# First modulation in eight groups of two K tiles, with the forget keys and the mix copies moved

## The reference, cut to what matters

```
mod    = silu(c) @ w_ada + b_ada              # one vector for latent, one for context
h      = x * (1 + sc1) + sh1                  # first modulation, both streams
u      = h @ w_in                             # values, keys, forget gates, queries, mix, gates
y_a    = rms_norm(gated linear recurrence(q, k, logf, v)) * silu(g)
y_b    = pooling(u);   y_c = attention(u)
x1     = layer_norm(alpha * x + g1 * (sum_j sigmoid(gate_j) * (y_j @ w_branch_j)) @ w_out)
out    = layer_norm(alpha * x1 + g2 * (relu(h2 @ w_ff1) ** 2) @ w_ff2),   h2 = x1 * (1 + sc2) + sh2
```

## Time and profile before

| | us |
|---|---|
| three runs | 1932.26, 1930.51, 1928.32 (median 1930.51) |
| profiled execution, its own time | 1933.53 |
| its span in the trace | 1931.7 |
| TensorE busy | 1870.1 |

### The profile page before, as it was taken

How to read it: one execution, slowest core, us unless ns; L and a number is a source line. 1 busy time by engine, 2 the same in 40 slices (tenths; PEclk the granted TensorE clock), 3 DMA queues, 4 the chain that set the end, 5 groups by cost and what they waited for, 6 DMA issues and landing times.

```text
span 1931.7 us, 23993 instructions
## 1 busy us (share of the span) xinstructions
PE 1870.1 (97%) x9784; PEld 1562.1 (81%) x9784; DVE 1283.3 (66%) x1454; ACT 810.2 (42%) x971; POOL 277.5 (14%) x165
## 2 busy tenths in 40 slices
PE   5999999999999999999999998999999999999997
PEld 1568987899999887878888887888888888888875
DVE  1236767785868766486676666786676567557786
ACT  1132234464555554444444434543344344434432
POOL 0000000004838253000010100120012001100100
PEclk8999999999999999999999999999999999999999
DMA  9956765554333454385676754565665565656642
GB/s 400 421 223 249 274 218 174 175 175 153 129 134 110 140 209 163 131 288 213 244 273 233 273 198 173 218 237 183 243 246 203 196 218 218 218 196 223 235 168 94
DMA packets 59598, 408.90 MB, mean 212 GB/s; under 512 B 6368, under 2 KB 9056, under 8 KB 10848
## 3 DMA queue, kind: packets, MB, share of 16 engines
q1 hardware_dynamic: 55008, 395.34, 56.0%
q10 hardware_dynamic: 4480, 12.02, 1.7%
HBM read 405.24 MB, written 2.10 MB: 211 GB/s over the span
## 4 chain that ended last, share of the span: by engine, by line
PE 87%; DVE 7%; DMA 2%; issue 1%; POOL 1%; DVEq 1%; ACT 1%; SPq 0%; ACTq 0%
PE main L1423 14%; PE main L1424 14%; PE main L1425 14%; PE side L1400 6%; PE main L1400 6%; PE main L1360 4%; PE main L1362 4%; PE main L1361 4%; PE side L1402 3%; PE main L1402 3%; DVE asum L940 2%; DMA raw<-in_w_ada 2%; PE main L1474 2%; DVE wlo L919 2%; PE main L1476 2%; PE main L1475 2%
## 5 line engine op out<-in xcount | busy, mean ns | idle before, releaser
L919 DVE TENSOR_TENSOR wlo<-raw,whi 128x1024 fp32r<-128x1024 f32 x548 | 703.8, 1311 | 356.4 <-ACT whi L457 355.7
L457 ACT CAST whi<-raw 128x1024 fp32r<-128x1024 f32 x548 | 570.3, 1052 | 745.0 <-PE main L1425 406.6
L1360 PE MATMUL main<-hCL,whi 128*128 128x256 f32 (+1 forms) x768 | 249.0, 324 | 8.0 <-ACT cq L623 4.4
L1362 PE MATMUL main<-hCL,wlo 128*128 128x256 f32 (+1 forms) x768 | 246.0, 320 | 0.0
L1361 PE MATMUL main<-hCL,whi 128*128 128x256 f32 (+1 forms) x768 | 245.8, 320 | 0.0
L940 DVE SCALAR_TENSOR_TENSOR asum<-raw,sm,asum 128x512 f32<-128x512 f32 x240 | 221.8, 924 | 19.5 <-issue 0.4
L1423 PE MATMUL main<-whi,hid 128*128 128x512 f32 x496 | 194.9, 393 | 2.8 <-DVE wlo L919 2.8
L1424 PE MATMUL main<-wlo,hid 128*128 128x512 f32 x496 | 193.1, 389 | 0.0
L1425 PE MATMUL main<-whi,hid 128*128 128x512 f32 x496 | 193.1, 389 | 0.0
L1400 PE MATMUL main<-h,whi 128*128 128x512 f32 x512 | 183.8, 403 | 4.8 <-DVE h L1255 2.5
L1400 PE MATMUL side<-h,whi 128*128 128x512 f32 x512 | 181.3, 399 | 0.0
(11 more groups left out here) (246 smaller groups left out, 2861.6 us busy)
## 6 DMA issues: line engine op xcount, KB each, us to landing
raw<-in_w_f SPq DMA_DIRECT2D x128, 1024.0 KB, 4.9
raw<-in_w_in SPq DMA_DIRECT2D x104, 1024.0 KB, 4.9
raw<-in_w_ada SPq DMA_DIRECT2D x96, 1024.0 KB, 5.5
raw<-in_w_br SPq DMA_DIRECT2D x24, 1024.0 KB, 4.9
raw<-in_w_out SPq DMA_DIRECT2D x16, 1024.0 KB, 4.8
xin<-in_xT SPq DMA_DIRECT2D x4, 1024.0 KB, 15.4
raw<-in_w_ck SPq DMA_DIRECT2D x4, 512.0 KB, 12.9
raw<-in_w_cv SPq DMA_DIRECT2D x2, 1024.0 KB, 4.9
```

Of the source, the lines that this page charges most:

```text
L457: nc.scalar.copy(half_at(q)[0], slots[slot][:, 2 * h:2 * h + 2]).then_inc(hi_made, 1)
L919: TT(half_at(q)[1], slots[slot][:, 2 * h:2 * h + 2], half_at(q)[0].bitcast(F32), ALU.subtract).then_inc(lo_made, 1)
L1360: mm(out, w_hi, x_hi, start=start, stop=False)
L1362: return mm(out, w_lo, x_hi, start=False, stop=stop)
```

## The change

`w_ada` is stored differently for its first 4096 columns (`w_ad1`): a chunk holds eight K tiles of 256 columns. `ada_chunk` makes eight matmuls of 256 columns in place of four of 512, two chunks make 256 sums, and two turns of two matmuls each serve a group of two K tiles, so that there are eight groups of four chunks. The load of the input goes in eight pieces. The values of group `g - 1` follow the four chunks of group `g`, one block behind each, and half of the keys of an earlier group follows them, ahead of the second turn. The last half of the values and the last keys come behind the loop. In the forget stage `keys_turned` and `states` come one chunk later each. In the mix stage the tanh and the copies stand ahead of the exponential of their step. The core of the diff:

```diff
@@ stream()
-    for kc in range(4):
+    for g in range(8):
         for k in range(4):
-            st.add("p", "ada", 8 * kc + k, "w_ada", 4 * kc + k)
...
+            if g and g % 2 == 0 and k == 2:
+                panel("vals", 0, g // 2, "w_in", 4 * PAN_AI + g // 2)
+            st.add("p", "ada", 4 * g + k, "w_ad1", 2 * (g + 8 * (k // 2)) + k % 2)
+        if g == 0:
+            panel("vals", 0, 0, "w_in", 4 * PAN_AI)
+        if g % 2:
+            st.add("s", "keys", g // 2, "w_ck", g // 2, halves=1)
@@ SyncE
-                if name == "ada" and k % 8 == 4:
...
+                if name == "ada" and k % 4 == 2:
+                    kt = 2 * (k // 4)
+                    sp.dma_start(xin[:, kt:kt + 2].rearrange("p k v t -> p (k v t)"),
+                                 xT[:, kt * 2 * T:(kt + 2) * 2 * T]).then_inc(x_in[k // 4], 16)
@@ ScalarE, opening
+            for g in range(8):
+                sums_out(2 * g)
+                if g and g % 2 == 0:
+                    split("vals", g // 2)
+                sums_out(2 * g + 1)
...
+                modulated(g)
+                if g == 0:
+                    split("vals", 0)
+                if g % 2:
+                    split("keys", g // 2)
@@ ScalarE, forget (the same shift by one in query: 0 and 1 become 1 and 2)
-                    if it >= 2 and k == 0:
+                    if it >= 2 and k == 1:
                         key_copy(it - 2)
-                    if it >= 2 and k == 1:
+                    if it >= 2 and k == 2:
                         state_copy(it - 2)
@@ ScalarE, mix (the same lines stood behind the exponential and the square before)
+                    if k == 3:
+                        for b in range(4):
+                            blk("mix", 12 * i, b)
+                            A(ya[:, i * 4 + b], main[:, b, 0:T], ACT.Tanh, scale=0.5).then_inc(gs_sig, 1)
+                    if k == 7:
+                        for b in range(4):
+                            blk("mix", 12 * i + 4, b)
+                            nc.scalar.copy(cq[:, i * 4 + b], main[:, b, 0:T]).then_inc(freed["A"], 1)
                     if k < 9:
                         act.wait_ge(lv_arg, i * 9 + k + 1)
@@ VectorE, opening
+            for g in range(8):
+                if g and g % 2 == 0:
+                    split("vals", g // 2)
+                mods_out(g)
+                modulate(g)
...
@@ TensorE, ada_chunk
-                for j in range(CK):
-                    group = slice(32 * j, 32 * j + 32)
-                    last = mm(side[group, 1], sR[:, k * CK + j], slots[slot][:, j], start=k == 0, stop=k == 3,
-                              tile_position=(0, 32 * j), skip_group_check=True)
+                for j in range(8):
+                    group, first = slice(32 * (j % 4), 32 * (j % 4) + 32), 256 * (j % 2)
+                    last = mm(side[group, 1, 256 * (p % 2):256 * (p % 2) + 256], sR[:, 8 * k + j],
+                              slots[slot][:, j // 2, first:first + 256], start=k == 0 and j < 4, stop=k == 1 and j >= 4,
+                              tile_position=(0, 32 * (j % 4)), skip_group_check=True)
@@ TensorE, opening
+            def keys_at(g):
+
+                n, pair = divmod(g - 2, 2)
+                if 0 <= n < 3:
+                    for b in range(2):
+                        key_block(n, 2 * b + pair)
+
+            for g in range(8):
                 for k in range(4):
...
+                    ada_chunk(4 * g + k)
+                    if k == 2:
+                        turn(2 * g)
+                    if g:
+                        n, h = divmod(g - 1, 2)
+                        inputs_ready(n, h)
+                        value_block("vals", n, h, k, half_ready("vals", n, h), 0)
+                keys_at(g)
+                turn(2 * g + 1)
@@ TensorE, between the chunks of the forget stage
                         if it:
                             ada_turn(3 + it)
                         if it >= 2:
-                            states(it - 2)
-                    if k == 3 and it:
-                        keys_turned(it - 1)
+                            keys_turned(it - 2)
+                    if k == 1 and it >= 2:
+                        states(it - 2)
@@ TensorE, query
                 if k == 0:
                     ada_turn(7)
+                    keys_turned(2)
+                if k == 1:
                     states(2)
```

More of the change, by code:

```diff
@@ L110, in panel @@
         while owed:
-            st.add("a", "sum", done, "w_ada", 4 * SUMS[done // 4] + done % 4)
+            st.add("a", "sum", done, "w_ada", 4 * (SUMS[done // 4] - 8) + done % 4)
             done, owed = done + 1, owed - 1
@@ L222, in panels @@
     four = (0, 1, 2, 3)
-    order = [half for n in range(4) for half in (("vals", n, 0), ("vals", n, 1), ("keys", n, 0))]
+    order = [("vals", 0, 0), ("vals", 0, 1)]
+    for n in range(1, 4):
+        order += [("vals", n, 0), ("keys", n - 1, 0), ("vals", n, 1)]
+    order.append(("keys", 3, 0))
     pn.together({"vals": four, "keys": ("side 2", "side 3")}, order, "A")
@@ L370, in build @@
         raw_full = [sem(f"raw_full{i}") for i in range(RAW + EXTRA)]
-        x_in = [sem(f"x_in{i}") for i in range(4)]
+        x_in = [sem(f"x_in{i}") for i in range(8)]
         hi_made, lo_made, ada_used, raw_used = sem("hi_made"), sem("lo_made"), sem("ada_used"), sem("raw_used")
@@ L485, in _ @@
             act.wait_ge(cst_in, 16)
[L486 to L498, removed]
+            for g in range(8):
[4 more added lines that the diff above has]
+                if g == 0:
+                    act.dma_start(mk_in[:].rearrange("p a b -> p (a b)"), masks).then_inc(mask_in, 16)
+                modulated(g)
+                if g == 0:
+                    split("vals", 0)
+                if g % 2:
+                    split("keys", g // 2)
             def values_out(t):
@@ L975, in lo @@
                        ALU.subtract).then_inc(h_lo, 1)
-                for k in range(4 * kc, 4 * kc + 4):
+                for k in range(2 * g, 2 * g + 2):
                     if k >= 2:
@@ L982, in modulate @@
                        ALU.mult, ALU.add).then_inc(h_tmp, 1)
-                    if k > 4 * kc:
+                    if k > 2 * g:
                         lo(k - 1)
[L985 to L994, removed]
-            split("keys", 3)
+                lo(2 * g + 1)
+            for g in range(8):
[3 more added lines that the diff above has]
+                modulate(g)
+                if g == 0:
+                    split("vals", 0)
+                if g % 2:
+                    split("keys", g // 2)
             split("vals", 4)
@@ L1461, in turn @@
                 pe.wait_ge(am_out, p + 1)
-                first = 32 * (p % 2) + 8 * (p // 2)
-                for b in range(4):
+                first = 32 * (p % 2) + 4 * (p // 2)
+                for b in range(2):
                     last = mm(side[:, 0, first + 2 * b:first + 2 * b + 2], am[:, p % 2, P * b:P * (b + 1)],
@@ L1544, in _ @@
             for n in range(3, 8):
-                for h in range(2):
+                for h in range(n == 3, 2):
                     if n == 3:
```

88 lines of the change are left out of this document (24 added, 64 removed).

## The result

The changed kernel takes 1936.12 us (median of 8 runs, 1933.44 to 1939.42) against 1930.07 for the kernel before (8 runs, 1927.99 to 1932.26), measured beside it. The ratio is 1.0033, 95% interval 1.0022 to 1.0044: slower by a third of a per cent, 6 us. I had forecast no change (1930.0). The profiled execution took 1938.00 us, its span is 1936.2, against 1933.53 and 1931.7 before.

What follows compares the result with a forecast made beforehand. TensorE, busy 97% of the span, was taken as the bound, so only its waits and low clock could pay. Opening +9.7, forget +1.0 and mix -11.2 gave -0.5: 1933.0 profiled, 1930 against the median, range 1919 to 1942.

Steps and rivals of the forecast that it cites:

- the mix term: Mix stage: moving tanh and copies ahead removes waits of 8.0 us and low clock of 3.2; -11.2 (-12 to -7).
- the clock's 3.2: Mix stage: one low-clock stretch in each half goes with its wait, 2 x 1.6 us gained.
- The opening's clock term: Opening: the clock falls behind three of six 2.4 us waits and the long one, 4 x 1.6 = +6.4 us.
- The order of the opening, at full clock: Opening: values start about 24 us, but new waits behind modulations give it back; end 148.5 against 147.2, +1.3.
- Rival A: Opening: waits behind the modulations do not lower the clock; sum -6.3, 1924 us, faster; chance 0.34.
- B: Opening: the clock falls at each of seven waits, 3.2 us lost each; sum +15.5, 1946 us; chance 0.16.
- The chunk (0.99): Opening: the new chunk of eight 256-column matmuls takes 0.99 us, as the columns streamed are the same.
- rival C: Opening: the new chunk is dearer, 0.86 us at each of 20 chunks, +17, 1947 us; chance 0.10.
- The forget keys (+1.0): Forget and query stages: keys turned a chunk later, net -0.2 plus clock +1.2; +1.0 us (-0.5 to +1.7).
- net of -0.2: Forget keys: 0.4 us won at each of three waits, the last turning's 1.0 added to the query stage.
- The clock's +1.2: Forget stage: first idle stretch grows from 2.6 to 3.3 us and may lower the clock; +1.2 (0 to 1.6).
- Rival D: Mix stage: GpSimd's arguments come as late as before, half of 11.2 becomes a new wait; +5.1, 1936 us; chance 0.04.

Runs made afterwards that it cites:

- the mix part alone: Kernel before with only the mix stage's tanh and copies moved ahead of the exponentials: 1924.45 us (6 runs), ratio 0.9962.
- the half-filled kernel: Changed kernel with 9 unused matmuls in each of six waits ahead of the values and 14 in the last: 1928.64 us, ratio 0.9978 to the kernel before.
- the filled kernels: Changed kernel with extra matmuls in the waits ahead of the values, three versions: 1927.83, 1929.05 and 1928.64 us, ratios 0.9982, 0.9982 and 0.9978.
- the opening alone: Kernel before with only the new opening, forget stage and mix as they were: 1939.05 us (5 runs), ratio 1.0040.

## Why the prediction was wrong

The sum was 9.7 + 1.0 - 11.2 = -0.5. In the profiled execution, cut as in the table, it was 12.3 + 2.2 - 8.7 - 1.3 = +4.5. The mechanisms were those forecast; the sizes of three terms were off, all the same way. The step that failed most is the mix term: 11.2 us were taken for it, and 8.7 came in the profile, 7.4 in the runs of the mix part alone and about 6.4 against a mix with one low-clock stretch. Two sizes in it were wrong, the new wait of 2.3 us that was put at nothing in the sum, and the clock's 3.2, counted in a profile with one stretch more than the two later ones. The opening's clock term, 6.4 forecast and 4.3 or 9.9 measured, is the second.

- **The order of the opening, at full clock (+1.3, and 2 for the start clock).** Right. TensorE's rows show the low clock up to about 28.6, though the windows read 1.00 there: the first value matmuls start 0.43 apart, those from 29.2 on 0.23 apart, so some 2 us of the 4.3 are lost, an estimate. The values start at 24.31 (about 24 forecast), the waits are six of 2.41 to 2.42 and one of 3.42 (six of 2.4 and one of 3.5). Without low clock the opening is 2.4 longer than before by the half-filled kernel; 3.3 was forecast.
- **The clock of the opening (+6.4).** Its size is what the prediction took from single rows, a loss of 1.6 at four of seven waits. The runs show 1.4 at three, or at seven counting two double stretches: 4.3 or 9.9 us. By the medians the filled kernels stand 7.9 to 9.1 us below the changed one on that chip. So the clock of the usual opening is about 2 us dearer than forecast, and the opening near +11 instead of +9.7 (2.4 + 8.5, an estimate). Rival A, with 1.6 lost, lies below the lower pattern, B (22.4) overstated the other: a wait is not charged in each round. The Trainium skill (TensorE: Matmul & The Clock Gate, HAM oscillation) says that a wait recurring in every round of a loop can cost the clock in every round. Here it did so in some rounds and some executions, with the same 2.41 us on both sides.
- **The chunk (0.99).** Right: 1.00 for the sixteen matmul rows of a new chunk at 66.70, above, where the eight rows of an old one took 0.99. That is 0.01 a chunk or 0.2 us for the 20, in place of rival C's 17.
- **The forget keys (+1.0).** The net of -0.2 failed. I let TensorE go on 0.4 earlier after each of the three waits, but the wait is 5.0 in all against 4.4, with the same turnings beside it. TensorE's timeline and windows of the kernel after at the first of them:

```profile
319.59 0.42 ACT L540 ACTIVATE kctx<-zL 128x256 f32<-128x256 f32 x1 [6.74 <-DVE zL L1032]
320.09 2.06 ACT L560 COPY z<-main 128x512 f32<-128x512 f32 x4
...
320.82 0.47 PE L1360 MATMUL main<-hCL,whi 128*128 128x512 f32 x1 [2.99 <-ACT z L560]
```

The copies do start at the exponential's end, and the wait is 2.99 where the old one was 2.60 with 1.1 us of turning behind it. The turnings' work was not saved, only moved behind the wait where no wait covers it. The two stages are some 0.5 longer without a low-clock stretch. The clock's +1.2 is 1.6 in the profile, but the kernels without the forget part meet that stretch too. Sum +2.2 in the profiled execution in place of +1.0; in the median it lies between 0.5 and that, and no run tells it from zero.
- **The mix (-11.2).** Two halves of one term. The waits of 8.0 all went, as forecast, and a new 2.3 came. I had named GpSimd as what is late next and put 1.5 for it in the range instead of the sum. Timelines of ScalarE and GpSimd after, first mix half:

```profile
496.00 0.39 ACT L608 ACTIVATE ya<-main 128x256 f32<-128x256 f32 x1 [2.74 <-PE main L1362]
...
498.83 1.91 ACT L616 ACTIVATE lv<-lv 128x2048 f32<-128x2048 f32 x1 [0.29 <-POOL lv L824]
...
522.61 1.74 POOL L821 TENSOR_TENSOR lv<-lf 128x512 f32<-128x512 f32 x1 [0.24 <-PE side L1630]
...
530.24 3.39 POOL L812 TENSOR_TENSOR lv<-lf,lfk 128x1024 f32<-128x1024 f32 x1
```

ScalarE now waits for TensorE ahead of the tanh, and GpSimd starts its rounds 7.6 us apart with 0.24 of rest. But the new waits are for a low half of a weight chunk (VectorE, up to 0.5, twice) and an issue gap at line 1641 (0.7 twice), so it was not GpSimd that they were put down to; what delays line 1641 the profile doesn't name, and no run took it apart. The other half is the clock, -3.2. The profile of before had two low-clock stretches in the mix, at 521.3 and 620.3, and the change took them both. The untouched mix in two later profiles had one. Windows of the mix, the kernel before, then the opening alone:

```profile
457.10:654.90 197.80, 189.76 (x1509) 186.44 (x1509) 145.54 (x129) 99.42 (x97) 108.92 (x67) 0.98 0.37 132
```

```profile
465.50:661.10 195.60, 188.17 (x1509) 184.91 (x1508) 142.48 (x128) 99.25 (x96) 107.03 (x67) 0.99 0.38 133
```

Busy time and waits add up: 189.76 + 8.0 before, 188.17 + 7.4 in the second, 186.76 + 2.3 after. Against the mix as it usually is the change gains about 6.4 us, 7.4 by the runs of the mix part alone. The 3.2 was real in the one execution that I read, and half of it was there in the two later profiles: it was counted in a profile that stood 3.0 above the median, and those 3.0 I took off again at the end.
- **The end.** An opening near +11, 0.5 to 2.2 for the forget part and -6.4 to -7.4 for the mix give +4 to +7, and +6 and +5 were measured. Rival D had the time (1936, at 4 in 100) by luck: it put the whole loss into the mix, where only the new wait and half of the clock's gain were right, and left the opening at its forecast price.

## What to carry to other kernels

Before a step is put ahead of another, ask which of the two somebody waits for: two key blocks ahead of one turn cost 21 to 24 us, two lines exchanged gave them back. A wait on TensorE of some 2 us costs more than its length, as the clock may fall behind it, so cut it below that, or fill it with work. And a term taken from low-clock stretches in one profile is a draw from several patterns: take the number of stretches from two or three profiles before it stands in a sum that comes out near zero.

## What the runs showed of the hardware

- The same wait, in the same kernel, lowers the clock in one execution and not in the next (2.41 us ahead of 56.60 and of 56.70). The shortest that did was 1.91 us in the opening and 1.82 us in the mix, where the clock fell 1.4 us after its end; none of the 0.91 us waits seen, nor the half-filled ones of up to 1.62, did.
- Each low-clock stretch was 3.4 us long or a multiple of it. It cost 1.4 us in the opening (9.9 for seven) and 1.6 in the forget stage.
- Extra matmuls of TensorE whose results nothing uses made a kernel 8 us faster (1936.95 and 1929.05 in two sets on one chip, 1.0032 and 0.9982 against the kernel before).
- Matmuls that start anew in one half of a PSUM bank reached the sums standing unfinished in the other half: the output was off by a relative 0.26, and with the start off, at the same places, it was whole. That it was the first chunk of the even pairs that got lost is inferred from the order, not shown.
